# Down products of two feed-forward layers by Strassen's seven block products

## Chip, cores and metric

One core of a Trainium2 chip runs the whole program. The metric is device time in microseconds. All arithmetic that matters here is on 32-bit data; each exact product is made of three TensorE passes (high x high, low x high, high x low), where high is the rounded part of a value (type fp32r) and low what the rounding left.

## Reference

One decoder layer on 1024 prompt tokens and 64 decode tokens, D_MODEL = 1024, D_FF = 2816:

```
def _swiglu(x, w_gate, w_up, w_down):
    return (jax.nn.silu(x @ w_gate) * (x @ w_up)) @ w_down
...
    x = _layer_norm(DN_ALPHA * x + 0.5 * _swiglu(x, f1g, f1u, f1d), ln_g[0], ln_b[0])
    m, s_new, new_k, new_v = _mixer(x, w_in, w_out, gn_w, sinks, ret_state, k_buf, v_buf)
    x = _layer_norm(DN_ALPHA * x + m, ln_g[1], ln_b[1])
    x = _layer_norm(DN_ALPHA * x + 0.5 * _swiglu(x, f2g, f2u, f2d), ln_g[2], ln_b[2])
```

`_mixer` (retention and window attention between two projections) lies between the layers that are changed.

## The kernel before

`ffn_stage` is one feed-forward layer, called twice. It goes over FT = 22 feature tiles of 128. For each tile f, TensorE makes the gate and then the up product of three token chunks (362, 364 and 362 tokens; 8 k-tiles x 3 passes = 24 matmuls each, so 48 per chunk), in two pairs of PSUM banks. ScalarE takes the silu of gate, VectorE multiplies it with up (`h_full`, L539), ScalarE rounds that (L308) and VectorE makes the low part (L547, and L549 for the decode rows). `down(f)` then multiplies the hidden tile with the down weights: for 8 token tiles and two halves of 512 columns 3 matmuls of 512 columns (L459 to L461), for the decode rows 2 x 2 (L456, L457), 52 in all, through four PSUM banks. VectorE adds each of the 18 results into `acc` in SBUF (L561). In the loop, a step is gate and up of tile f, then `down(f - 1)`. The last two tiles, A and B, are interleaved by hand: their down products go together in PSUM (`last_down`, L483 to L487), tile by tile, with the layer norm's steps behind each tile (`norm_tile`: sums, ScalarE `deviation`, GpSimd `gain` (L714), VectorE `shift` (L739), TensorE `turn` (L751), ScalarE `high`, VectorE `low` (L769)).

Weights come by the one DMA queue of SyncE: gate, up and down tile of 512 KB each, requested when the down products of an earlier tile are done. ScalarE rounds each tile (`round_part`, L293), GpSimd subtracts to get its low part in place (`split`, L375, 1024 columns). During the first layer's start SyncE also loads the first two weight tiles (Q, K) of the retention projection and the norm's rows (`between_loads`); ScalarE and GpSimd round and split them there (`RetentionPrefetch`, L838 and L843). After the layer, `retention_projection_stage` loads, rounds (L900) and splits (L955) the other two, V and GATE. Every engine runs its own list in order; the list orders are those of the functions `sync`, `scalar`, `gpsimd`, `tensor`, `vector`.

Of the kernel before, what the change touches and what calls it, by code (L numbers as in the profile page):

```python
# [22 lines left out]
F32 = mybir.dt.float32  # L23
# [5 lines left out]
P = 128  # L29
# [4 lines left out]
SEQ = 1024  # L34
# [152 lines left out]
class FfnBuffers:  # L187


    def __init__(self, tag, even, odd, work):  # L190

        self.hi, self.raw, self.low = [], [], []
        for s, place in enumerate((even, odd)):
            self.hi.append([place.put(f"{tag}w_hi{s}{j}", [P, KT, P], F32R) for j in range(3)])
            pairs = [place.put_raw_and_low(f"{tag}w{s}{j}", [P, KT, P]) for j in range(3)]
            self.raw.append([raw for raw, _ in pairs])
            self.low.append([low for _, low in pairs])
        self.h_hi = [work.put(f"{tag}h_hi{s}", [P, TOK + 2 * DEC], F32R) for s in range(2)]
        self.h_lo = [work.put(f"{tag}h_lo{s}", [P, SEQ], F32R) for s in range(2)]
        self.silu = work.put(tag + "silu", [P, 3, CW])  # L200
        self.h_full = work.put(tag + "h_full", [P, 3, CW])


def ffn_stage(core, tag, buffers, w_in, fold, acc, xh, xl, wait_x, acc_ready, norm, room=None, banks_free=None,
              first_norm=None, load=None, between_loads=lambda sp: None, prefetch=None):

    w_hi, w_raw, w_lo = buffers.hi, buffers.raw, buffers.low
    h_hi, h_lo, silu, h_full = buffers.h_hi, buffers.h_lo, buffers.silu, buffers.h_full
    GATE, UP, DOWN = range(3)
    NC_ = len(CHUNKS)  # L210
    DOWNS = 2 * TOKEN_TILES
    sem = lambda n: core.semaphore(tag + n)
    gate_ps, up_ps, down_ps = core.banks[0:4:2], core.banks[1:4:2], core.banks[4:8]
    staged = [sem(f"staged{j}") for j in range(3)]
    gu_hi, down_hi = sem("gu_hi"), sem("down_hi")
    gu_split, down_split = sem("gu_split"), sem("down_split")
    gate_done, up_done = sem("gate_done"), sem("up_done")
    silu_done = sem("silu_done")
    pair_free = sem("pair_free")
    h_hi_done, h_lo_done = sem("h_hi_done"), sem("h_lo_done")  # L220
    down_done, down_free = sem("down_done"), sem("down_free")

    A, B = FT - 2, FT - 1

    LAST = [(A, 0), (A, 1), (B, 0), (B, 1), (A, 2), (B, 2)]

# [27 lines left out]

    def load_part(sp, f, s, j):
        src = w_in[f, :, j, :] if isinstance(f, int) else w_in[bass.ds(f, 1), :, j, :].rearrange("a p n -> (a p) n")
        sp.dma_start(flat(w_raw[s][j]), src).then_inc(staged[j], 16)

    def sync_early(sp, j):
        load_part(sp, 0, 0, j)  # L260

    def sync(sp):
        if room:
            sp.wait_ge(*room)
            load_part(sp, 0, 0, DOWN)
# [28 lines left out]

    def scalar_early(act, j):
        round_part(act, 0, 0, j)

    def scalar(act):
        def silu_chunk(f, s, c):
            a, b = CHUNKS[c]  # L300
            act.wait_ge(gate_done, number(f, c) + 1)
            act.activation(silu[:, buffer_of(f, s, c), 0:b - a], gate_ps[pair_of(f, s, c)][:, 0:b - a],  # L302
                           ACT.Silu).then_inc(silu_done, 1)

        def round_h(f, s, c):
            a, b = CHUNKS[c]
            act.wait_ge(pair_free, 2 + number(f, c) + 1)
            act.activation(h_hi[s][:, a:b], h_full[:, buffer_of(f, s, c), 0:b - a],  # L308
                           ACT.Copy).then_inc(h_hi_done, 1)

        def silu_and_round(f, s, c):
            silu_chunk(f, s, c)
            round_h(f, s, c)

        def step(f, s):
            silu_and_round(f, s, 0)
            round_part(act, f + 1, 1 - s, GATE)
# [5 lines left out]
        def first_step():
            silu_and_round(0, 0, 0)
            round_part(act, 1, 1, GATE)
            round_part(act, 1, 1, UP)
            silu_and_round(0, 0, 1)
            round_part(act, 0, 0, DOWN)
            silu_and_round(0, 0, 2)

        def first_step_with_norm():
            silu_chunk(0, 0, 0)
            first_norm.high(act, TOKEN_TILES - 3)
            round_h(0, 0, 0)
            first_norm.high(act, TOKEN_TILES - 2)
            round_part(act, 1, 1, GATE)
            silu_chunk(0, 0, 1)
            first_norm.high(act, TOKEN_TILES - 1)
            round_h(0, 0, 1)
            round_part(act, 1, 1, UP)  # L340
            round_part(act, 0, 0, DOWN)
            silu_and_round(0, 0, 2)

        if first_norm:
            first_step_with_norm()
        else:
            first_step()
        if prefetch:
            prefetch.scalar_early(act)
        tiles(act, step)  # L350
        round_part(act, B, 1, GATE)
        round_part(act, B, 1, UP)
        silu_and_round(A, 0, 0)
        round_part(act, A, 0, DOWN)
        silu_and_round(A, 0, 1)
        silu_and_round(B, 1, 0)
        round_part(act, B, 1, DOWN)
        silu_and_round(B, 1, 1)
        norm.deviation(act, 0)
        norm.deviation(act, 1)  # L360
        silu_and_round(A, 0, 2)
# [4 lines left out]
        silu_and_round(B, 1, 2)  # L366
# [5 lines left out]
    def split(pool, f, s, j):  # L372
        done, rounded, n = (down_split, down_hi, f + 1) if j == DOWN else (gu_split, gu_hi, 2 * f + j + 1)
        pool.wait_ge(rounded, n)
        pool.tensor_tensor(flat(w_lo[s][j]), flat(w_raw[s][j]), flat(w_hi[s][j]).bitcast(F32),  # L375
                           ALU.subtract).then_inc(done, 1)
# [5 lines left out]
    def gpsimd(pool):  # L382
        def step(f, s):
            split(pool, f + 1, 1 - s, GATE)
            split(pool, f + 1, 1 - s, UP)
            split(pool, f, s, DOWN)

        step(0, 0)
        if prefetch:
            prefetch.gpsimd_early(pool)  # L390
        tiles(pool, step)
        split(pool, B, 1, GATE)
        split(pool, B, 1, UP)
        split(pool, A, 0, DOWN)
        split(pool, B, 1, DOWN)
# [3 lines left out]
    def tensor(pe):  # L399
        def gate_or_up(f, s, c, j):  # L400
            a, b = CHUNKS[c]
            ps, done = ((gate_ps, gate_done), (up_ps, up_done))[j]
# [7 lines left out]
            mm.then_inc(done, 1)  # L410

        def first_gate():
# [14 lines left out]
            mm.then_inc(gate_done, 1)  # L427
# [7 lines left out]
        def high_and_low(s):  # L435

            return h_hi[s][:, SEQ:SEQ + P], h_hi[s][:, TOK:TOK + P]

        def down(f, s):
            pe.wait_ge(down_split, f + 1)  # L440
            for t in range(TOKEN_TILES):
                if t in (0, 2, 5):
                    pe.wait_ge(h_lo_done, number(f, chunk_of_tile(t)) + 1)
                if t == BLOCKS - 1:
                    pe.wait_ge(gu_split, min(2 * f + 6, 2 * FT) if isinstance(f, int) else 2 * f + 6)
                if t == BLOCKS:
                    pe.wait_ge(down_split, f + 2)
                u = slice(P * t, P * t + P)
                for half in range(2):
                    n, d = 2 * t + half, slice(512 * half, 512 * half + 512)  # L450
                    pe.wait_ge(down_free, DOWNS * f + n + 1 + DOWNS - 4)
                    out = down_ps[(n + 2 * s) % 4]
                    hi, lo = flat(w_hi[s][DOWN])[:, d], flat(w_lo[s][DOWN])[:, d]
                    if t == BLOCKS:
                        both = h_hi[s][:, SEQ:SEQ + P]
                        pe.matmul(out, both, hi, start=True, stop=False)  # L456
                        pe.matmul(out, both, lo, start=False, stop=True).then_inc(down_done, 1)  # L457
                    else:
                        pe.matmul(out, h_hi[s][:, u], hi, start=True, stop=False)  # L459
                        pe.matmul(out, h_lo[s][:, u], hi, start=False, stop=False)  # L460
# [1993 lines left out]
```

## Time and profile before

| | before |
|---|---|
| runs (3) | 2143.75 us median, 2142.12 to 2144.74 |
| profiled execution | 2143.15 us, its span 2141.3 us |
| TensorE busy | 2096.4 us, 98% of the span |
| VectorE, ScalarE, GpSimd busy | 910.3, 505.7 and 520.6 us |
| granted TensorE clock, mean | 0.994 of full speed |

The profile is one execution. Matmul ends in it are modelled, so the cost of a matmul is best read as the distance between the starts of two neighbours. In the rows, PE is TensorE, DVE VectorE, ACT ScalarE, POOL GpSimd, SPq the DMA queue of SyncE.

### The profile page before, as it was taken

The page shows a single profiled execution, that of the slowest core. Times are in us where ns is not written, and L with a number is a line of the kernel's source. Part 1 is how long each engine was busy: PE and PEld are TensorE (multiplying, and loading weights), DVE is VectorE, ACT ScalarE, POOL GpSimd, SP SyncE. Part 2 cuts the span into 40 slices and gives each one's busy share as a digit, 9 for nine tenths or more (in the row PEclk, how much of TensorE's full clock was granted, in tenths as well). Part 3 has the DMA queues.
Part 4 walks back from the last instruction along what each step waited for, and adds up shares of the span by engine and source line. Part 5 has one row for each costly group of instructions (what it writes and reads, how often), then busy time and mean ns, then how long its engine had stood idle before and what let it go on. Part 6 is the DMA issues. An engine that isn't in the chain of part 4 may idle for free.

```text
span 2141.3 us, 31092 instructions
## 1 busy us (share of the span) xinstructions
PE 2096.4 (98%) x11989; PEld 1927.4 (90%) x11989; DVE 910.3 (43%) x1686; ACT 505.7 (24%) x887; POOL 520.6 (24%) x261
## 2 busy tenths in 40 slices
PE   8999999999999999999998999999999999999997
PEld 8999999999999989999796667999999999999996
DVE  5534353535353552101656536444444443434346
ACT  4111111111112153111136344211111111111115
POOL 3221212121212132221454223212121212121213
PEclk9999999999999999999999999999999999999999
DMA  7010101010101112111123011110101010101012
GB/s 287 30 59 29 59 29 59 29 59 31 57 33 56 40 50 74 50 39 34 62 86 141 1 50 60 34 60 29 59 29 59 29 59 29 59 29 59 30 59 84
DMA packets 38074, 118.40 MB, mean 55 GB/s; under 512 B 6271, under 2 KB 10879, under 8 KB 37759
## 3 DMA queue, kind: packets, MB, share of 16 engines
q1 hardware_dynamic: 38015, 117.58, 15.3%
q8 instruction: 41, 0.67, 0.1%
q14 instruction: 18, 0.15, 0.0%
HBM read 106.29 MB, written 11.27 MB: 55 GB/s over the span
## 4 chain that ended last, share of the span: by engine, by line
PE 95%; DVE 2%; issue 1%; DMA 1%; ACT 1%; POOL 0%; SPq 0%; DVEq 0%; ACTq 0%
PE bank L119 20%; PE bank L121 20%; PE bank L120 20%; PE bank L461 7%; PE bank L460 7%; PE bank L459 7%; PE bank L1863 2%; PE bank L1865 2%; PE bank L1864 2%; PE bank L1833 1%; PE bank L457 1%; PE bank L456 1%; PE bank L751 1%; PE bank L486 1%; PE bank L1185 1%
## 5 line engine op out<-in xcount | busy, mean ns | idle before, releaser
L119 PE MATMUL bank<-x_hi,f_w_hi 128*128 128x362 f32 (+1 forms) x2104 | 689.2, 328 | 1.8 <-DVE x_low L162 1.8
L121 PE MATMUL bank<-x_hi,f_w_low 128*128 128x362 f32 (+1 forms) x2104 | 689.1, 328 | 0.0
L375 POOL TENSOR_TENSOR f_w_low<-f_w_raw,f_w_hi 128x1024 fp32r<-128x1024 f32 x132 | 316.6, 2415 | 1182.5 <-ACT f_w_hi L293 1182.5
L561 DVE TENSOR_TENSOR acc<-bank,acc 128x512 f32<-128x512 f32 x720 | 467.8, 686 | 6.7 <-PE bank L461 4.4
L539 DVE TENSOR_TENSOR f_h_full<-bank,f_silu 128x362 f32<-128x362 f32 (+1 forms) x132 | 70.6, 535 | 815.3 <-PE bank L121 813.0
L119 PEld LDWEIGHTS bank<-x_hi,f_w_hi 128*128 128x128 f32 x2104 | 395.9, 188 | 3.9 <-issue 2.0
L121 PEld LDWEIGHTS bank<-x_hi,f_w_low 128*128 128x128 f32 x2104 | 396.2, 188 | 0.0
L120 PE MATMUL bank<-x_lo,f_w_hi 128*128 128x362 f32 (+1 forms) x1056 | 345.5, 327 | 0.0
L120 PE MATMUL bank<-x_low,f_w_hi 128*128 128x362 f32 (+1 forms) x1048 | 343.0, 327 | 0.0
L461 PE MATMUL bank<-f_w_low,f_h_hi 128*128 128x512 f32 x640 | 250.4, 391 | 0.0
L459 PE MATMUL bank<-f_w_hi,f_h_hi 128*128 128x512 f32 x640 | 250.0, 391 | 0.3 <-DVE acc L561 0.3
L460 PE MATMUL bank<-f_w_hi,f_h_lo 128*128 128x512 f32 x640 | 250.3, 391 | 0.0
L302 ACT ACTIVATE f_silu<-bank 128x362 f32<-128x362 f32 (+1 forms) x132 | 62.5, 474 | 678.3 <-PE bank L121 678.2
L120 PEld LDWEIGHTS bank<-x_lo,f_w_hi 128*128 128x128 f32 x1056 | 198.7, 188 | 1.0
L120 PEld LDWEIGHTS bank<-x_low,f_w_hi 128*128 128x128 f32 x1048 | 197.2, 188 | 0.8
L308 ACT ACTIVATE f_h_hi<-f_h_full 128x362 fp32r<-128x362 f32 (+1 forms) x132 | 67.0, 508 | 528.6 <-DVE f_h_full L539 528.6
L461 PEld LDWEIGHTS bank<-f_w_low,f_h_hi 128*128 128x128 f32 x640 | 120.2, 188 | 25.9
L459 PEld LDWEIGHTS bank<-f_w_hi,f_h_hi 128*128 128x128 f32 x640 | 120.3, 188 | 25.3 <-DVE f_h_lo L547 0.7
L460 PEld LDWEIGHTS bank<-f_w_hi,f_h_lo 128*128 128x128 f32 x640 | 120.2, 188 | 24.5
L293 ACT ACTIVATE f_w_hi<-f_w_raw 128x1024 fp32r<-128x1024 f32 x132 | 133.9, 1044 | 33.7 <-DMA f_w_raw<-ffn_in 33.7
L119 PE MATMUL bank<-x_hi,rp_w_hi 128*128 128x362 f32 (+1 forms) x384 | 126.9, 331 | 0.0
L120 PE MATMUL bank<-x_low,rp_w_hi 128*128 128x362 f32 (+1 forms) x384 | 126.1, 328 | 0.0
(207 smaller groups left out, 2215.7 us busy)
## 6 DMA issues: line engine op xcount, KB each, us to landing
f_w_raw<-ffn_in SPq DMA_DIRECT2D x132, 512.0 KB, 4.4
rp_w_raw<-w_ret_in SPq DMA_DIRECT2D x16, 512.0 KB, 3.5
acc<-x_rows_in SPq DMA_DIRECT2D x2, 2048.0 KB, 11.1
kept_rows<-acc SPq DMA_DIRECT2D x8, 512.0 KB, 2.9
ow_raw<-w_out_in SPq DMA_DIRECT2D x8, 512.0 KB, 6.6
y_out<-acc SPq DMA_DIRECT2D x8, 512.0 KB, 2.7
n_rows<-ln_rows_in SPq DMA_DIRECT2D x6, 512.0 KB, 5.1
gp_stage<-w_att_in SPq DMA_DIRECT2D x4, 512.0 KB, 3.5
```

The source lines that it names most:

```text
L119: pe.matmul(out, wh, xh, start=first, stop=False)
L120: pe.matmul(out, wh, xl, start=False, stop=False)
L121: return pe.matmul(out, wl, xh, start=False, stop=last)
L293: act.activation(flat(w_hi[s][j]), flat(w_raw[s][j]), ACT.Copy).then_inc(down_hi if j == DOWN else gu_hi, 1)
L302: act.activation(silu[:, buffer_of(f, s, c), 0:b - a], gate_ps[pair_of(f, s, c)][:, 0:b - a], ACT.Silu).then_inc(silu_done, 1)
L308: act.activation(h_hi[s][:, a:b], h_full[:, buffer_of(f, s, c), 0:b - a], ACT.Copy).then_inc(h_hi_done, 1)
L375: pool.tensor_tensor(flat(w_lo[s][j]), flat(w_raw[s][j]), flat(w_hi[s][j]).bitcast(F32), ALU.subtract).then_inc(done, 1)
L459: pe.matmul(out, h_hi[s][:, u], hi, start=True, stop=False)
L460: pe.matmul(out, h_lo[s][:, u], hi, start=False, stop=False)
L461: pe.matmul(out, h_hi[s][:, u], lo, start=False, stop=True).then_inc(down_done, 1)
L539: dve.tensor_tensor(h_full[:, at, 0:b - a], up_ps[pair_of(f, s, c)][:, 0:b - a], silu[:, at, 0:b - a], ALU.mult).then_inc(pair_free, 1)
L561: dve.tensor_tensor(acc[:, t, d], down_ps[(n + 2 * s) % 4][:, :], acc[:, t, d], ALU.add).then_inc(down_free, 1)
```

## The change

The 22 feature tiles are worked in 11 pairs. For ten of them the 2 x 2 block product (two halves of 512 tokens by two feature tiles, times two feature tiles by two halves of 512 output columns) is made by Strassen's seven block products. Each product is a *group* of four token tiles x 3 matmuls of 512 columns; the decode rows get 8 matmuls. The five sums of hidden blocks are made by VectorE, the five sums of down weights by GpSimd; sums and blocks are rounded by ScalarE, and their low parts are subtracted by VectorE (hidden) and GpSimd (weights). VectorE adds or subtracts a product from PSUM into one or two places of `acc`. The groups of the pair before lie between half chunks (24 matmuls of gate or of up) of the current pair. The last pair (A, B) keeps `last_down`, in another order with its last chunks. Gate and up tiles are requested when the tile that held their buffer is done, down tiles two at a time when the pair's last group is done. Down tiles of the first pair are no longer loaded ahead. The prefetch of the retention weights and the norm's rows are loaded at the end of layer 1, and only Q is rounded and split there; K waits for the end of the products, and its split stands ahead of `norm.gain(7)`. Silu is written into `h_full` in place. Buffers are laid out anew. The core of the diff; first the seven products, each with its hidden block, its weight block, the parts it waits for, and its targets (rows, columns, sign):

```
+SEVEN = [
+    (H1, D1, 1, 1, [(0, 0, ADD), (1, 1, ADD)]),
+    (H2, D2, 1, 2, [(1, 0, ADD), (1, 1, SUB)]),
+    (H3, D3, 2, 3, [(0, 1, ADD), (1, 1, ADD)]),
+    (H4, D4, 3, 3, [(0, 0, ADD), (1, 0, ADD)]),
+    (H5, D5, 4, 4, [(0, 1, ADD), (0, 0, SUB)]),
+    (H6, D6, 4, 5, [(1, 1, ADD)]),
+    (H7, D7, 4, 5, [(0, 0, ADD)]),
+]
```

SyncE, for each pair q with f = 2q:

```
+            sp.wait_ge(gu_done, 12 * q)
+            load_part(sp, f + 1, 1, GATE)
+            load_part(sp, f + 1, 1, UP)
+            sp.wait_ge(gu_done, 12 * q + 6)
+            load_part(sp, f + 2, 0, GATE)
+            load_part(sp, f + 2, 0, UP)
+            sp.wait_ge(down_done, SEVENS * q)
+            load_down(sp, f, 0)
+            load_down(sp, f + 1, 1)
```

ScalarE, `round_pair`:

```
+            act.wait_ge(h_ready, (SUMS + LOWS) * q + 2)
+            high(cut(buffers.h_hi, 2, 4), cut(buffers.h_raw, 2, 4))
+            act.wait_ge(pair_free, 2 + number(f, 2) + 1)
+            high(cut(buffers.h_hi, 0, 1), h_full[:, 0, 0:HALF])
+            high(cut(buffers.h_hi, 1, 2), h_full[:, 1, HALF:SEQ])
+            act.wait_ge(down_split, (DOWN_SUMS + DOWN_LOWS) * q + DOWN_SUMS)
+            weights(cut(buffers.ds_hi, 0, 1), cut(buffers.ds_raw, 0, 1))
+            weights(cut(buffers.d_hi, 0, 1), cut(buffers.d_raw, 0, 1))
+            weights(cut(buffers.ds_hi, 1, 3), cut(buffers.ds_raw, 1, 3))
+            act.wait_ge(h_ready, (SUMS + LOWS) * q + SUMS)
+            high(buffers.hs_hi[:, :], buffers.hs_raw[:, :])
+            weights(cut(buffers.d_hi, 3, 4), cut(buffers.d_raw, 3, 4))
+            weights(cut(buffers.d_hi, 1, 3), cut(buffers.d_raw, 1, 3))
+            high(packs[:, 0:6 * DEC].rearrange("p (s n) -> p s n", s=2)[:, :, 0:DEC], h_full[:, :, SEQ:TOK])
+            high(pack(2, 0, DEC), dec_sum[:, :])
```

GpSimd, for each pair (`sums`: five of 512 columns; `split_down`: 512, 512, 1024, 512 and 1024 columns):

```
+            split(pool, f + 1, 1, GATE)
+            split(pool, f + 1, 1, UP)
+            split(pool, f + 2, 0, GATE)
+            split(pool, f + 2, 0, UP)
+            sums(q)
+            split_down(q)
```

TensorE, for each pair, with p = q - 1:

```
+            gate_up(f, 0, 0)
+            gate_up(f, 0, 1, between=lambda: group(p, 0))
+            group(p, 1)
+            gate_up(f, 0, 2, between=lambda: group(p, 2))
+            group(p, 3)
+            gate_up(f + 1, 1, 0, between=lambda: group(p, 4))
+            decode(p)
+            gate_up(f + 1, 1, 1, between=lambda: group(p, 5))
+            group(p, 6)
+            gate_up(f + 1, 1, 2)
```

VectorE, `sums_and_lows`:

```
+            dve.wait_ge(pair_free, 2 + number(f, 2) + 1)
+            combine(raw(H1), a11, a22, ADD)
+            combine(raw(H2), a21, a22, ADD)
+            combine(raw(H5), a11, a12, ADD)
+            combine(raw(H6), a21, a11, SUB)
+            combine(raw(H7), a12, a22, SUB)
+            combine(dec_sum[:, :], h_full[:, 0, SEQ:TOK], h_full[:, 1, SEQ:TOK], ADD)
+            low(1, cut(buffers.h_lo, 2, 4), cut(buffers.h_raw, 2, 4), cut(buffers.h_hi, 2, 4))
+            low(2, cut(buffers.h_lo, 0, 1), a11, cut(buffers.h_hi, 0, 1))
+            low(3, cut(buffers.h_lo, 1, 2), a22, cut(buffers.h_hi, 1, 2))
+            low(4, buffers.hs_lo[:, :], buffers.hs_raw[:, :], buffers.hs_hi[:, :])
+            low(6, two[:, :, DEC:2 * DEC], h_full[:, :, SEQ:TOK], two[:, :, 0:DEC])
+            low(6, pack(2, DEC, 2 * DEC), dec_sum[:, :], pack(2, 0, DEC))
```

VectorE, for each pair:

```
+            h_chunk(f, 0, 0)
+            add_group(p, 0)
+            h_chunk(f, 0, 1)
+            add_group(p, 1)
+            add_group(p, 2)
+            h_chunk(f, 0, 2)
+            add_group(p, 3)
+            add_group(p, 4)
+            h_chunk(f + 1, 1, 0)
+            add_decode(p)
+            add_group(p, 5)
+            h_chunk(f + 1, 1, 1)
+            add_group(p, 6)
+            h_chunk(f + 1, 1, 2)
+            sums_and_lows(q, f + 1)
```

TensorE, the last phase, from tile A on:

```
+        gate_up(A, 0, 0)
+        gate_up(A, 0, 1, between=lambda: group(p, 0))
+        two_groups(1)
+        gate_up(B, 1, 0, between=lambda: group(p, 3))
+        group(p, 4)
+        decode(p)
+        gate_up(B, 1, 1, between=lambda: two_groups(5))
+        gate_up(A, 0, 2)
         last_down(0)
         last_down(1)
```

## Rows read from the trace of the kernel before

**Rows 1.** The page: span, busy times, chain by engine, granted clock.
```profile
span 2141.3 us, 31092 instructions
PE 2096.4 (98%) x11989; PEld 1927.4 (90%) x11989; DVE 910.3 (43%) x1686; ACT 505.7 (24%) x887; POOL 520.6 (24%) x261
PEclk9999999999999999999999999999999999999999
PE 95%; DVE 2%; issue 1%; DMA 1%; ACT 1%; POOL 0%; SPq 0%; DVEq 0%; ACTq 0%
```
**Rows 2.** Waits from 100 to 740 us (us in total, times, longest).
```profile
DVE f_h_full L539 <- PE bank L121: 344.0, 53, 7.0
...
PEld bank L459 <- issue: 0.2, 1, 0.2
```
**Rows 3.** Windows on TensorE: stretch, us, busy (matmuls recorded), clock, DMA share, GB/s.
```profile
407.47:415.15 7.68, 7.68 (x49) 1.00 0.00 0
415.15:426.98 11.83, 11.83 (x55) 1.00 0.00 0
426.98:434.98 8.00, 8.00 (x50) 1.00 0.55 197
...
1527.91:1540.00 12.09, 12.09 (x54) 1.00 0.00 0
```
**Rows 4.** Instruction groups by shape: busy us, mean ns; idle before.
```profile
L561 DVE TENSOR_TENSOR acc<-bank,acc 128x512 f32<-128x512 f32 x720 | 467.8, 686 | 6.7 <-PE bank L461 4.4 <-DVE acc L561 0.2
...
L547 DVE TENSOR_TENSOR f_h_lo<-f_h_full,f_h_hi 128x362 fp32r<-128x362 f32 x44 | 24.2, 550 | 25.3 <-ACT f_h_hi L308 25.3
...
L1139 POOL TENSOR_TENSOR rt_q_dec<-ret_q,rt_q_decay 128x512 f32<-128x512 f32 x8 | 10.2, 1270 | 35.9 <-DVE ret_v_tok L1046 23.3 <-PE bank L1185 11.9 <-DMA rt_own<-own_in 0.8
```
**Rows 5.** Timeline of VectorE and GpSimd, 36 to 60 us: start, us, instruction.
```profile
38.78 2.29 DVE L167 TENSOR_SCALAR acc<-acc 128x4096 f32<-128x4096 f32 x1 [0.59 <-DMA acc<-x_rows_in]
40.99 4.52 DVE L168 TENSOR_SCALAR acc<-acc 128x4096 f32<-128x4096 f32 x1
45.44 2.89 DVE L169 TENSOR_SCALAR acc<-acc 64x1024 f32<-64x1024 f32 x1
...
54.51 2.79 DVE L547 TENSOR_TENSOR f_h_lo<-f_h_full,f_h_hi 128x364 fp32r<-128x364 f32 x1 [0.58 <-ACT f_h_hi L308]
...
40.96 6.82 POOL L843 TENSOR_TENSOR rp_w_low<-rp_w_raw,rp_w_hi 128x1024 fp32r<-128x1024 f32 x2 [7.22 <-ACT rp_w_hi L838]
52.14 7.41 POOL L375 TENSOR_TENSOR f_w_low<-f_w_raw,f_w_hi 128x1024 fp32r<-128x1024 f32 x3 [4.36 <-ACT f_w_hi L293]
```
**Rows 6.** Timeline, GpSimd and VectorE at 807 to 811 us.
```profile
807.56 2.52 POOL L714 TENSOR_TENSOR acc<-acc,n_rows 128x1024 f32<-128x1024 f32 x1 [2.33 <-ACT acc L698]
807.74 0.68 DVE L578 SCALAR_TENSOR_TENSOR acc<-bank,acc 128x512 f32<-128x512 f32 x1
...
810.20 1.28 DVE L739 SCALAR_TENSOR_TENSOR acc<-acc,n_stats,n_rows 128x1024 f32<-128x1024 f32 x1 [0.85 <-POOL acc L714]
```
**Rows 7.** DMA issues after a tile: the queue's timeline, and us to landing.
```profile
427.32 1.38 SPq L257 DMA_DIRECT2D f_w_raw<-ffn_in  x3
...
f_w_raw<-ffn_in SPq DMA_DIRECT2D x3, 512.0 KB, 4.3
```
**Rows 8.** Timeline at the end of layer 1: last weight split, table load.
```profile
749.36 2.40 POOL L375 TENSOR_TENSOR f_w_low<-f_w_raw,f_w_hi 128x1024 fp32r<-128x1024 f32 x1 [25.51 <-ACT f_w_hi L293]
...
765.46 1.28 ACT L302 ACT_TABLE_LOAD   x1
```
**Rows 9.** Timeline at the start of the retention projection.
```profile
810.79 1.04 ACT L900 ACTIVATE rp_w_hi<-rp_w_raw 128x1024 fp32r<-128x1024 f32 x1
...
812.78 3.23 DVE L739 SCALAR_TENSOR_TENSOR acc<-acc,n_stats,n_rows 128x1024 f32<-128x1024 f32 x1
816.92 0.69 DVE L769 TENSOR_TENSOR x_low<-bank,x_hi 128x512 fp32r<-128x512 f32 x1 [0.90 <-ACT x_hi L762]
...
817.76 1.60 PE L751 MATMUL bank<-small,acc 128*128 128x128 f32 x8 [2.15 <-DVE x_low L769]
```

More of the change, by code:

```diff
@@ L196, in __init__ @@
             self.raw.append([raw for raw, _ in pairs])
             self.low.append([low for _, low in pairs])
[L198 to L201, printed above, removed]
+        self.packs = pack.put(tag + "h_packs", [P, 2 * 3 * DEC + 2 * DEC], F32R)
+        self.h_full = main.put(tag + "h_full", [P, 2, TOK])
@@ L323, in first_step @@
[L323 to L332, printed above, removed]
+            if c == 0:
+                act.wait_ge(down_done, DONE - SEVENS + 16)
+            rows = min(b, SEQ)
+            x = act.activation(h_row(buffers.h_hi, s, a, rows), h_full[:, s, a:rows], ACT.Copy)
@@ L348, in scalar @@
+        round_last_down(A, 0)
+        round_last_down(B, 1)
+        round_last(B, 1, 1)
+        round_last(A, 0, 2)
         if prefetch:
             prefetch.scalar_early(act)
[L350 to L358, printed above, removed]
         norm.deviation(act, 0)
@@ L433, in gate_up @@
             gate_or_up(f, s, c, UP)
[L435 to L460, printed above, removed]
-                        pe.matmul(out, h_hi[s][:, u], lo, start=False, stop=True).then_inc(down_done, 1)
@@ new lines, in decode @@
+        def decode(q):
+            pe.wait_ge(h_ready, (SUMS + LOWS) * q + SUMS + LOWS)
+            for half, parts in enumerate((((2, D2), (1, D4)), ((2, D5), (0, D3)))):
+                n = 4 * FIFTH + half
+                pe.wait_ge(down_free, SEVENS * q + SEVENS + n - 3)
+                out = down_ps[n % 4]
+                for i, (s, which) in enumerate(parts):
+                    both = pack(s, 0, 2 * DEC)
+                    pe.matmul(out, both, slot(buffers.d_hi, buffers.ds_hi, which), start=i == 0, stop=False)
+                    mm = pe.matmul(out, both, slot(buffers.d_lo, buffers.ds_lo, which), start=False, stop=i == 1)
+                mm.then_inc(down_done, 1)
@@ L563, in add_down, with add @@
-        def add_down(f, s, ns=range(DOWNS)):
-            for n in ns:
-                add_part(f, s, n)
+                x = dve.tensor_tensor(pack(s, DEC, 2 * DEC), h_full[:, s, SEQ:TOK], pack(s, 0, DEC).bitcast(F32),
+                                      ALU.subtract)
+            x.then_inc(h_ready, 1)
+        def add(q, n, t, half, op, last):
+            d = slice(HALF * half, HALF * half + HALF)
+            x = dve.tensor_tensor(acc[:, t, d], acc[:, t, d], down_ps[n % 4][:, :], op)
+            if last:
+                x.then_inc(down_free, 1)
```

515 lines of the change are left out of this document (320 added, 195 removed).

## Prediction

> **What bounds the kernel now.** I read the page first: TensorE is busy 98% of the span at full granted clock, VectorE 43%, ScalarE and GpSimd 24% each, and the chain that ended last is TensorE for 95% [rows 1]. Then the waits of a long stretch of the first feed-forward layer: TensorE's own waits add up to 0.2 us in 640, and what the other engines wait for is mostly TensorE's results [rows 2]. So time falls where TensorE issues less, and rises where a new wait makes TensorE stop. Then come the windows, which give the cost of a matmul as the distance between starts: the 52 products of one down tile take 11.83 us, 0.2275 each; a 48-matmul chunk takes 7.68 us (0.160 each) or 8.00 (0.1667) [rows 3]. In the second layer 52 products took 12.09 us in one tile [rows 3].
>
> **What is removed.** Two feature tiles now cost 52 x 2 = 104 down matmuls. Seven block products of 4 token tiles x 3 passes are 84, and the decode rows 2 x 4 = 8: 92. That is 12 fewer for each of 10 pairs in each of 2 layers, 240 in all, at 0.2275 us: **-54.6 us**. The last pair of a layer stays as it is. Without stalls a pair would take 96 x (0.160 + 0.1667 + 0.160) + 92 x 0.2275 = 46.7 + 20.9 = 67.7 us, against two times 35.5 now (11.83 + 7.68 + 8.00 + 8.00). DMA bytes are the same. The buffers lie elsewhere, and the rate of one shape differs by 2 to 4% between places in rows 3 without my knowing why: plus or minus 10 us, taken at 0.
>
> **What is added.** Per pair, VectorE adds 48 + 2 products into `acc` instead of 36: 14 more at 0.686 us [rows 4], 9.6 us on an engine that idles over half the time. A product with two targets takes VectorE about 0.64 + 0.61 = 1.25 us and TensorE 3 x 0.2275 = 0.68; a group (2.7) with the half chunk behind it (3.8) leaves 6.5 us for 5.0 of adds, so inside a pair the adds are covered once they have begun in time. What must be in time is the block at the end of a pair, `sums_and_lows`: twelve VectorE instructions that read two SBUF tensors, and beside it five sums and five splits of down weights on GpSimd, 9 x 512 columns or 1024. Durations: 362 columns took VectorE 0.550 us, 512 took 0.686 [rows 4], 1024 took 1.28 [rows 6]; in a row of them each occupies VectorE about 0.08 less than it takes, so I count 0.61 for 512, 1.14 for 1024, 1.68 for 1536 and 0.15 for 64 or 128. The five sums of 512, the small sum, the lows of 1024, 512, 512, 1536 and the packed rows occupy VectorE 7.3 us in all. GpSimd takes 1.27 us for 512 columns [rows 4], 2.40 for 1024 [rows 8].
>
> **The two engines exclude each other there.** VectorE's 4096-column scaling took 2.29 us alone and 4.52 behind a GpSimd split that began 0.03 us before; the 1024-column one behind it took 2.89, because the second GpSimd split, waiting since, went first; the two splits took 6.82 instead of 2 x 2.40. A 364-column `h_lo` subtraction took 2.79 us instead of 0.55 under three GpSimd splits, which together took 7.41 [rows 5]. An addition from PSUM at 807.74 took its usual 0.68 under a running GpSimd instruction [rows 6]. I read this as: an instruction with two SBUF inputs waits for the end of the other engine's one, and the two then alternate. The Trainium skill, "SBUF — State Buffer", section "SBUF: two separate sides", says the same, that the pair of ports is locked for a whole instruction and the loser fully blocks; by that rule too this change is dearer than its busy times, and the trace agrees with the 2.79 and 4.52 us above; without the rule the sum would be rival 2's. In the kernel before, the meetings are rare, since splits run where VectorE adds from PSUM or idles.
>
> **The schedule of a pair, from rows.** Zero is the start of the next pair's first gate chunk. The last group ends at -7.7 (one chunk of 0.160 x 48). The DMA queue starts its issues 0.34 us after the tile's end, the second 0.47 later, and one of 512 KB landed 4.3 us after issue as the median of three [rows 7]; both down loads are there at -7.7 + 5.1 = -2.6. GpSimd's sums run from then, three of them done at +1.1. VectorE's last `h_full` ends at 0.8. From here the two alternate: sum 1 1.1 to 1.7, GpSimd's fourth to 2.8, sum 2 to 3.3, its fifth to 4.4, sums 3 to 5 to 6.1. ScalarE has rounded the first weight block at 5.9, so GpSimd takes 6.0 to 7.2; small sum to 7.3; split 2 to 8.4; the first low (1024) 8.4 to 9.5; split 3 (1024) to 11.7; low 2 to 12.2; split 4 to 13.3; low 3 to 13.8; split 5 (1024) to 16.1; low 4 (1536) to 17.6. By now ScalarE has also rounded the next gate and up tiles (0.95 each from 12.8), so GpSimd goes on with two splits of 2.3 us, and VectorE's two packed-row instructions wait for one each: it is free at **22.3**. In that order VectorE waited some 14 us for 7.3 of work. It then does `h_full` of chunk 0, which is queued behind, and only at 22.8 the first add, although TensorE gave group 0 from 11.7 to 14.4. The up half chunk covers until 18.4. Group 1 needs the banks of group 0: its products can start at 24.1, 25.4, 26.6, 27.9 and the last ends at 28.6 instead of 21.1. **Stall 7.4 us per pair.** After it the adds are in time again. The stall recurs as long as both engines have work, for pairs 2 to 10, that is 9 times in a layer; the first pair's down weights are early and it costs 0.8.
> Sum: 18 x 7.4 + 2 x 0.8 = **+134.8 us**. Bounds: if VectorE wins the fewest turns (the overlap of start-up, about 0.1 us each, taken as none) 9.5 us a pair; if the loads land 0.3 us sooner, GpSimd's fifth sum ends before sum 3 wants, the first low is done at 7.3, and one GpSimd instruction fewer stands ahead of low 4: VectorE is free at 17.8, stall 2.9. If there is no exclusion at all it is free at about 11 and the stall is 0.
>
> **The ends of the layers.** (a) In the last phase groups 1 and 2 stand back to back, paced by 1.25 us a product: 2.7 us more each layer (1.4 without exclusion). (b) The last down weights are loaded after group 6, but ScalarE rounds them behind the silu of the chunk before `last_down(0)`: gate end +3.84, silu +0.7, two roundings, two splits of 2.41, about 10.5 us after the start of a chunk that lasts 7.7: 2.8 us each layer. Before, this split ran from 749.36 to 751.8, ahead of its use at 755 [rows 8]. (c) The last silu now waits behind `deviation(3)` and a table load of 1.28 us [rows 8] while its up half is shorter: 1.9 us in the first layer, 1.3 in the second. (d) At the change to the retention projection the second weight tile (K) is rounded and split only after the last product, and its split stands ahead of `norm.gain(7)` on GpSimd. Now: gain(7) 807.56 to 810.1, then shift(7) 810.20, ending with the last shift at 816.0 and x_low at 816.92 [rows 6, 9]. After: rounding of K ends where V's ended, 811.85; its split to 814.4; gain(7) to 816.8; the splits of V and GATE, long rounded, follow it and take turns with the last three VectorE instructions of 1.28: shift(7) after V's at 819.1 to 820.2, the next after GATE's at 822.5 to 823.6, the last shift to 824.9, x_low of tile 6 to 825.7. TensorE's turn of tile 7, now at 817.76, would start at about 826.4: +8.7 us. Norm rows, prefetch and `kept_rows` stay covered; they are loads of 512 KB that have over 10 us. Sum: 5.4 + 5.6 + 3.2 + 8.7 = **+22.9**.
> At the starts nothing: down weights no longer come early and the GpSimd splits of the prefetch, under which the scaling ran slow, are gone; what TensorE waits for there is x, whose loads stand ahead as before.
>
> **Sum.** -54.6 + 134.8 + 22.9 = +103.1 us on the profiled execution's own 2143.15 us (its span is 2141.3; the median of the runs is 2143.75): **2246 us**.
>
> **Rivals.** (1) *The stall stays small*: the same alternation in its better order, 2.9 us a pair: -54.6 + 53.8 + 22.9 = +22.1, 2165 us. For it: the two orders are parted by some 0.3 us in the landing. Against: 5.1 us is the measured landing. 23%. (2) *Covered*: the sums and splits do not collide (or VectorE keeps its turn), it is free by 18.4, when group 1 needs the first bank, and the stall is 0: -54.6 + 2.8 + 5.6 + 3.2 + 8.7 = -34.3, **2109 us**, faster. It decides when VectorE leaves the block within 17 us of zero: then the count of matmuls rules. For it: VectorE has only 42 us of work in 68 (50 adds at 0.64, six `h_full` at 0.5, the block's 7.3). Against: rows 5. 22%. (3) *Between the two*, 1 to 2 us a pair, 2115 to 2150 us: 8%. (4) *VectorE becomes late through the whole pair* (9.5 us a pair, or adds of over 0.75): 2260 to 2285: 5%.
>
> **Chances and range.** The forecast 42%, its own range 2215 to 2260. Slower by over 0.2% (about 4.3 us, what this measurement can tell from none): 42 + 20 + 5 = 67%; within 0.2%: 5%; faster 28% (all of rival 2, most of 3). The range from 2105 to 2260 takes in the forecast, rivals 1 and 3 and the upper part of 2.
>
> **What the new profile would show.** Group matmuls 240 fewer at 0.227 us; VectorE additions at about 0.69; `hs` and `h` sums and lows with means far over 0.69 (waits inside); a gap on TensorE ahead of group 1, about 7 us, "idle, released by VectorE acc", once in each pair, with the period near 75 us; one gap of about 3 us ahead of the first `last_down`. I am wrong if the sums on VectorE have their bare durations, if the period is near 68, or if the gap sits at another group (then the adds, not the exclusion, are the bound).

## The result, and the profile after

The changed kernel takes 2267.87 us (median of 4 runs, 2260.48 to 2269.38) against 2144.24 us for the one before (4 runs, 2142.12 to 2146.21): a ratio of 1.057, 95% interval 1.0545 to 1.0595. It is slower, as forecast, but by 124 us instead of 103, and 8 us above the top of my range. The profiled execution is the fastest of the four, 2260.48 us.

The page of the changed kernel, beside [rows 1]: span, busy times, granted clock and the chain by engine.

```profile
span 2258.7 us, 31130 instructions
PE 2101.8 (93%) x11749; PEld 1914.3 (85%) x11749; DVE 1416.2 (63%) x2046; ACT 549.5 (24%) x947; POOL 800.9 (35%) x421
PEclk9999999999999999999999999999999999999999
PE 75%; DVE 17%; issue 6%; ACT 1%; DMA 1%; POOL 1%; DVEq 0%; SPq 0%; ACTq 0%
```

TensorE has its 240 matmuls less (11989 to 11749), yet its busy time grew by 5 us, and its share of the chain fell from 95% to 75%, with VectorE now at 17%. Over the whole run the mean granted clock is 0.965, against 0.994 before. The waits from 120 to 750 us (TensorE's own were 0.2 us in the 640 us of [rows 2]):

```profile
DVE f_h_full L689 <- PE bank L121: 113.4, 34, 7.1
...
DVE acc L736 <- PE bank L580: 57.0, 37, 4.0
...
PE bank L578 <- DVE acc L736: 41.2, 9, 6.0
```

The groups by shape, beside [rows 4]:

```profile
L736 DVE TENSOR_TENSOR acc<-acc,bank 128x512 f32<-128x512 f32 x1000 | 623.3, 680 | 149.6 <-PE bank L580 135.2 <-PE bank L592 11.5 <-DVE acc L736 0.4
...
L704 DVE TENSOR_TENSOR f_h_low<-f_h_full,f_h_hi 128x512 fp32r<-128x512 f32 x40 | 82.1, 2091 | 0.0
...
L704 DVE TENSOR_TENSOR f_hs_low<-f_hs_raw,f_hs_hi 128x1536 fp32r<-128x1536 f32 x20 | 75.7, 3785 | 3.8 <-ACT f_hs_hi L369 3.8
...
L704 DVE TENSOR_TENSOR f_h_packs<-f_h_full,f_h_packs 128x128 fp32r<-128x128 f32 x20 | 49.0, 2449 | 0.0
L578 PE MATMUL bank<-f_d_hi,f_h_hi 128*128 128x512 f32 x80 | 48.8, 611 | 99.1 <-DVE acc L736 99.0
```

The thousand additions from PSUM kept their price, 680 ns against 686 before. The instructions with two SBUF inputs did not: 2.09 us for 512 columns, 2.45 us for 128. They are long themselves and do not stand behind missing inputs: VectorE's idle time ahead of these three groups is 3.8 us in the whole run. The last line holds the stall: the products that read `d_hi` and `h_hi` are those of group 1 (4 in each of 20 pairs), and they stood 99 us behind VectorE's additions.

One pair in the timeline of VectorE and GpSimd (`f_h_packs` holds the decode rows). Its zero, the first matmul of the next pair's first gate chunk, is 433.27:

```profile
434.04 2.79 DVE L700 TENSOR_TENSOR f_h_raw<-f_h_full 128x512 f32<-128x512 f32 x2
436.75 2.98 DVE L700 TENSOR_TENSOR f_hs_raw<-f_h_full 128x512 f32<-128x512 f32 x3
439.66 1.32 DVE L700 TENSOR_TENSOR f_dec_sum<-f_h_full 128x64 f32<-128x64 f32 x1
440.91 2.33 DVE L704 TENSOR_TENSOR f_h_low<-f_h_raw,f_h_hi 128x1024 fp32r<-128x1024 f32 x1
443.16 4.58 DVE L704 TENSOR_TENSOR f_h_low<-f_h_full,f_h_hi 128x512 fp32r<-128x512 f32 x2
447.67 3.97 DVE L704 TENSOR_TENSOR f_hs_low<-f_hs_raw,f_hs_hi 128x1536 fp32r<-128x1536 f32 x1
451.56 2.44 DVE L704 TENSOR_TENSOR f_h_packs<-f_h_full,f_h_packs 128x128 fp32r<-128x128 f32 x1
453.92 2.35 DVE L704 TENSOR_TENSOR f_h_packs<-f_dec_sum,f_h_packs 128x64 fp32r<-128x64 f32 x1
456.20 0.52 DVE L689 TENSOR_TENSOR f_h_full<-bank,f_h_full 128x362 f32<-128x362 f32 x1
...
430.75 3.83 POOL L485 TENSOR_TENSOR f_ds_raw<-f_d_raw 128x512 f32<-128x512 f32 x3 [21.06 <-DMA f_d_raw<-ffn_in]
...
449.98 6.21 POOL L471 TENSOR_TENSOR f_w_low<-f_w_raw,f_w_hi 128x1024 fp32r<-128x1024 f32 x2
```

GpSimd's sums begin at -2.5 (forecast -2.6), VectorE's block starts at 0.8 (0.8) and lets `h_full` through at 22.9 (22.3). A packed row of 64 columns takes 2.35 us there, about the length of one GpSimd split of 1024 columns (2.40 in [rows 8]). TensorE in the same pair, as windows (stretch, length, busy of PE, PEld, DVE, ACT, POOL, clock, DMA share, GB/s):

```profile
451.90:457.97 6.07, 0.32 (x3) 0.02 (x2) 6.07 (x6) 0.47 (x1) 4.30 (x2) 0.95 0.00 0
457.97:460.60 2.63, 2.63 (x6) 1.98 (x7) 2.63 (x5) 0.00 (x0) 0.00 (x0) 0.50 0.00 0
460.60:466.00 5.40, 5.40 (x30) 4.78 (x30) 5.40 (x10) 0.00 (x0) 0.00 (x0) 0.98 0.00 0
```

TensorE stands still until group 1 at 457.97, 24.7 after zero (24.1). Then the granted clock is 0.50, its lower level of 1.2 GHz, after 5.8 us in which TensorE had waited. This was not in my prediction. Here it lasts 2.6 us and group 1 takes 4.39 us; in other pairs the wait is as long, the clock is at 0.50 through all of group 1, and group 1 takes 5.3 us. The interval between two blocks is 68.98 us for the first in layer 1 and 69.03 in layer 2, 70.46 once, and 76.5 to 77.9 in the other 15; behind the last block of each layer there is no next one to measure to, and group 1 waited there too.

### The profile page after: what moved, and what is told of

It is laid out like the page before. It is cut to its first block, busy times and chain, and to the rows that moved or that the text cites. A ratio compares the mean times of both kernels' runs of the same rounds, so it can differ in the third digit from the quotient of the medians.

```text
span 2258.7 us, 31130 instructions
## 1 busy us (share of the span) xinstructions
PE 2101.8 (93%) x11749; PEld 1914.3 (85%) x11749; DVE 1416.2 (63%) x2046; ACT 549.5 (24%) x947; POOL 800.9 (35%) x421
## 4 chain that ended last, share of the span: by engine, by line
PE 75%; DVE 17%; issue 6%; ACT 1%; DMA 1%; POOL 1%; DVEq 0%; SPq 0%; ACTq 0%
PE bank L119 15%; PE bank L121 15%; PE bank L120 15%; PE bank L578 6%; PE bank L579 5%; PE bank L580 5%; DVE f_h_packs L704 4%; DVE f_hs_low L704 3%; DVE f_h_low L704 2%; DVE acc L736 2%; PE bank L2076 2%; PE bank L2078 1%; PE bank L2077 1%; DVE f_hs_raw L700 1%; DVE f_h_raw L700 1%
## 5 line engine op out<-in xcount | busy, mean ns | idle before, releaser
L736 DVE TENSOR_TENSOR acc<-acc,bank 128x512 f32<-128x512 f32 x1000 | 623.3, 680 | 149.6 <-PE bank L580 135.2
L471 POOL TENSOR_TENSOR f_w_low<-f_w_raw,f_w_hi 128x1024 fp32r<-128x1024 f32 x88 | 236.4, 2705 | 514.6 <-ACT f_w_hi L354 504.7
L364 ACT ACTIVATE f_h_full<-bank 128x362 f32<-128x362 f32 (+1 forms) x132 | 62.5, 474 | 1137.4 <-PE bank L121 964.5
L689 DVE TENSOR_TENSOR f_h_full<-bank,f_h_full 128x362 f32<-128x362 f32 (+1 forms) x132 | 70.2, 532 | 314.7 <-PE bank L121 311.4
L485 POOL TENSOR_TENSOR f_ds_raw<-f_d_raw 128x512 f32<-128x512 f32 x60 | 76.1, 1297 | 380.3 <-DMA f_d_raw<-ffn_in 380.3
L578 PE MATMUL bank<-f_d_hi,f_h_hi 128*128 128x512 f32 x80 | 48.8, 611 | 99.1 <-DVE acc L736 99.0
L121 PE MATMUL bank<-x_hi,rp_w_low 128*128 128x362 f32 (+1 forms) x384 | 127.2, 331 | 0.0
L503 POOL TENSOR_TENSOR f_ds_low<-f_ds_raw,f_ds_hi 128x512 fp32r<-128x512 f32 (+1 forms) x40 | 100.2, 2505 | 52.7 <-ACT f_ds_hi L372 52.7
L503 POOL TENSOR_TENSOR f_d_low<-f_d_raw,f_d_hi 128x512 fp32r<-128x512 f32 (+1 forms) x60 | 114.7, 1925 | 0.0
L578 PE MATMUL bank<-f_ds_hi,f_h_hi 128*128 128x512 f32 x240 | 94.9, 396 | 1.9 <-DVE acc L736 1.9
```

Source lines behind the costliest of these rows:

```text
L121: return pe.matmul(out, wl, xh, start=False, stop=last)
L485: pool.tensor_tensor(out, x, y, op).then_inc(down_split, 1)
L503: pool.tensor_tensor(lo[:, u], raw[:, u], hi[:, u].bitcast(F32), SUB).then_inc(down_split, 1)
L578: pe.matmul(out, high, w_h, start=True, stop=False)
L689: dve.tensor_tensor(h_full[:, s, a:b], up_ps[pair_of(f, s, c)][:, 0:b - a], h_full[:, s, a:b], ALU.mult).then_inc(pair_free, 1)
L736: x = dve.tensor_tensor(acc[:, t, d], acc[:, t, d], down_ps[n % 4][:, :], op)
```

## The experiments

Line numbers of the variants can lie a few higher than those above. Each ratio is to the kernel before on the same chip.

### 1. GpSimd's share taken away

```
-                pool.tensor_tensor(out, x, y, op).then_inc(down_split, 1)
+                pool.tensor_tensor(out[:, 0:n], x[:, 0:n], y[:, 0:n], op).then_inc(down_split, 1)
...
-                u = slice(HALF * a, HALF * b)
+                u = slice(HALF * a, HALF * a + few if few else HALF * b)
...
-            w_h, w_l = slot(buffers.d_hi, buffers.ds_hi, d), slot(buffers.d_lo, buffers.ds_lo, d)
+            w_h, w_l = slot(buffers.d_hi, buffers.ds_hi, d), slot(buffers.d_hi, buffers.ds_hi, d)
```

`n` and `few` are 8, but for the first pair of a layer, which keeps its full widths. TensorE reads the rounded weights in place of their low parts, so this kernel leaves work out of GpSimd's share and none out of VectorE's or TensorE's.

> Work is left out: in the pairs of the loop GpSimd's five sums and five splits of down weights work on 8 columns instead of 512 or 1024, and TensorE reads the rounded weights where it read their low parts; counts of instructions and waits stay. My theory (the two engines exclude each other on instructions with two SBUF inputs) expects VectorE's block of sums and lows at 8 to 9 us instead of 22.2, no wait of TensorE ahead of group 1, the granted clock at 1.00 through the pairs, and a period of 69.0 us as in the first pair instead of 76.5 to 77.9: 18 x about 8 less, 2120 to 2130 us. The rival, that the 50 additions from PSUM are too many for VectorE, expects the wait to stay, above 2250 us. A third reading, that ScalarE's roundings set the block, expects the block above 12 us and a time between.

Measured: 2117.83 us, ratio 0.9878 (0.9861 to 0.9894) to the kernel before, 2 us below the range of my theory. Groups by shape, and one whole pair as a window:

```profile
L700 DVE TENSOR_TENSOR f_hs_raw<-f_h_full 128x512 f32<-128x512 f32 x60 | 37.8, 686 | 0.0
L704 DVE TENSOR_TENSOR f_hs_low<-f_hs_raw,f_hs_hi 128x1536 fp32r<-128x1536 f32 x20 | 37.2, 1860 | 25.1 <-ACT f_hs_hi L369 25.1
...
L704 DVE TENSOR_TENSOR f_h_low<-f_h_full,f_h_hi 128x512 fp32r<-128x512 f32 x40 | 25.8, 686 | 0.0
```

```profile
406.20:475.25 69.05, 69.05 (x382) 65.04 (x381) 42.24 (x69) 13.81 (x21) 13.75 (x14) 1.00 0.14 46
```

VectorE's instructions are untouched and have their bare durations again: 686 ns where 2091 stood, the block 9.2 us instead of 22.2, the period 69.05, the clock 1.00. With all 1000 additions in place there is no stall, so their number is not the bound. Nor are ScalarE's roundings, with which the block would have stayed above 12 us. ScalarE's `hs_hi` holds VectorE up by 1.25 us a pair (25.1 in 20), which costs TensorE nothing. The Trainium skill, "SBUF — State Buffer", section "SBUF: two separate sides", has the pair of ports locked for a whole instruction, the loser fully blocked; the trace of the changed kernel agrees with 2.35 us for 64 columns beside a 1024-column split.

### 2. Part of the block moved behind group 0's additions

```
             h_chunk(f, 0, 0)
             add_group(p, 0)
+            last_lows(p)        # low(4, ...), low(6, ...), low(6, ...) out of sums_and_lows
             h_chunk(f, 0, 1)
```

ScalarE's silu of (f, 1) then waits only for low 3, that of (f, 2) for all.

> The last three subtractions of VectorE's block (low of 1536 columns, two packed rows) are issued in the next pair, after h_full of chunk 0 and the additions of group 0; nothing is left out. If the stall comes only from what stands ahead of those additions, they begin at about 14.5 + 0.5 us after zero instead of 23, group 1 finds its banks, the stall goes, the clock stays at 1.00 and the period is 69 to 70: 2120 to 2135 us. Rival: the subtractions now wait for GpSimd's gate and up splits in the middle of the additions of groups 0 and 1, and the wait only moves to group 2, with 2 to 4 us a pair: 2160 to 2200 us. If the additions themselves were the bound, nothing changes: above 2250 us.

Measured: 2148.21 us, ratio 1.0021 (1.0012 to 1.0031), 120 us less than the changed kernel. `h_full` passes 14.6 us after zero. Periods are 70.1 to 70.9 us, and the time is 13 us above the upper end of the better expectation: VectorE in the next pair shows why.

```profile
426.13 4.86 DVE L745 TENSOR_TENSOR acc<-acc,bank 128x512 f32<-128x512 f32 x8
430.91 3.47 DVE L724 TENSOR_TENSOR f_hs_low<-f_hs_raw,f_hs_hi 128x1536 fp32r<-128x1536 f32 x1
434.30 0.28 DVE L724 TENSOR_TENSOR f_h_packs<-f_h_full,f_h_packs 128x128 fp32r<-128x128 f32 x1
434.50 0.21 DVE L724 TENSOR_TENSOR f_h_packs<-f_dec_sum,f_h_packs 128x64 fp32r<-128x64 f32 x1
...
435.08 9.64 DVE L745 TENSOR_TENSOR acc<-acc,bank 128x512 f32<-128x512 f32 x16
```

The low of 1536 columns now met GpSimd's gate and up splits (3.47 us instead of 1.86), group 1's additions began at 435.1, and three products of group 2 waited 0.4 us each for a bank: the group took 4.35 us where 2.80 is its length without waits. The granted clock stayed at 1.00. The rival's mechanism was there, at 1.0 to 1.9 us a pair instead of 2 to 4.

### 3. One target for each product

```
-            targets = SEVEN[m][4]
+            targets = SEVEN[m][4][:1]
```

> Work is left out: each product is added into one target only, so that VectorE has 28 + 2 additions in a pair instead of 48 + 2. By my theory the block is untouched at 22.2 us and only the pacing of group 0's additions is halved: products of group 1 can start 0.64 apart instead of 1.25, the stall is about 5 us instead of 7.5, and with 18 pairs and the ends the time is 2205 to 2230 us. If the number of additions were the bound, the stall would go wholly: about 2125 us.

Measured: 2250.41 us in one run. Neither number was met. Against the reading that additions are the bound it is plain: 40% of them gone, and periods still of 75.6 to 77.4. But my own theory expected 2205 to 2230. The windows of the wait and of group 1:

```profile
453.60:459.10 5.50, 0.14 (x1) 0.00 (x0) 5.50 (x5) 0.47 (x1) 4.34 (x2) 0.90 0.00 0
459.12:464.40 5.28, 5.28 (x12) 4.12 (x13) 4.15 (x7) 0.00 (x0) 0.00 (x0) 0.50 0.00 0
```

I had the stall shrink because group 1's products could follow each other 0.64 us apart. They could, as far as banks go, but the clock had fallen in the wait, and twelve matmuls took 5.28 us at 0.50 instead of 2.80. In the changed kernel banks that come free 1.25 us apart and the half clock cover the same time, so removing the first brings little: the long periods are 76.5 us in the mean instead of 77.2, and what is gained is that group 1 starts some 0.6 us sooner. I had expected about 2.5 us a pair.

### 4. The order at the ends of the layers

```
         silu_chunk(B, 1, 1)
-        silu_chunk(A, 0, 2)
         round_last_down(A, 0)
         round_last_down(B, 1)
+        silu_chunk(A, 0, 2)
...
+        norm.gain(pool, 7)
         split(pool, 0, K)
-        norm.gain(pool, 7)
```

> Two changes of order at the ends of layers, nothing left out: ScalarE rounds the last down weights ahead of the silu of chunk (A, 2), and GpSimd does gain(7) ahead of the split of K. My terms (b) and (d) were 2.8 us a layer and 8.7 us once. In the trace of the changed kernel TensorE waits 2.5 and 2.3 us at the first last down product and 5.4 + 3.0 us at the turns of tiles 7 and 8 and K, against 2.2 before. So this should give back 4.8 + 5 to 8: 10 to 13 us, 2255 to 2258 us. Rival: the waits at the change to the retention projection come from the lateness of the whole norm, and only 4 to 6 us come back: 2262 to 2264 us.

Measured: 2256.01 us (ratio 1.0521, 1.0503 to 1.0538): 11.9 less than the changed kernel by the medians, as expected. TensorE's waits, 770 to 890 us:

```profile
PE bank L578 <- DVE acc L736: 6.3, 4, 5.7
PE bank L119 <- POOL rp_w_low L1167: 3.4, 1, 3.4
PE bank L968 <- DVE acc L956: 3.1, 3, 1.1
PE bank L615 <- issue: 0.7, 1, 0.7
```

The first line is group 1 of the last pair and not an end. The wait for the last down weights fell from 2.5 to 0.7 us (in layer 2 from 2.3 to nothing) and that of 5.4 us for `x_low` is gone; the one for K's low part (3.0 before, 3.4 now) remains, since ScalarE rounds K only then.

### 5. The block's tail behind group 1, with the ends mended

As in 2, but `last_lows(p)` stands behind `add_group(p, 1)`; with the edits of 4.

> The last three subtractions of VectorE's block now stand after the additions of group 1 in the next pair, and the two changes of order at the ends (rounding of the last down weights ahead of the silu of (A, 2), gain(7) ahead of K's split) are in too; nothing is left out. With them ahead of the additions of group 1 the pairs took 70.2 to 70.9 us, and TensorE waited three times 0.4 us in group 2. If those 3.9 us of subtractions are the whole rest of the stall, the period falls to 69.0, 18 x 1.4 = 25 us, and the ends give some 10: 2148 - 35 = 2113 us, 2108 to 2120. Rival: the additions of group 2, queued behind them now, come late for group 3, and the 0.4 us waits only move there: 2135 to 2142 us.

Measured: **2106.00 us** (5 runs, 2105.38 to 2107.31), ratio 0.9825 (0.9812 to 0.9839), 37 us faster than the kernel before and 2 us below the range I had given. TensorE's waits from 120 to 750 us:

```profile
PE bank L617 <- issue: 0.8, 1, 0.8
PE bank L580 <- DVE acc L745: 0.6, 3, 0.2
```

### 6. TensorE's loop elsewhere in the program

The kernel of experiment 5 with 64 fulfilled waits ahead of `pairs(pe, step)`.

> The kernel with lows after group 1 and mended ends, with 64 further waits on TensorE's queue ahead of the loop over pairs in each layer, all long fulfilled; they only move the loop's instructions in the program. It asks what makes the same matmul start every 0.160 us in one stretch and every 0.1667 in another. If the place of an instruction in the program sets it, the borders between 0.160 and 0.1667 (in layer 1 the gate half of chunk 2 is fast, the up half slow) shift or vanish, and the period of 69.0 changes by 0.3 to 1.5 us. If data, buffers or the other engines set it, pattern and period stay (69.0) and the time is within 4 us of the kernel without the waits.

Measured: 2107.83 us (ratio 0.9832, 0.9817 to 0.9847). The period stays 69.04 and 69.10, and in layer 1 the gate half of chunk 2 takes 3.84 us and its up half 4.00, as without the waits. Only the first interval of each layer is 1.0 us longer, which is the whole of the difference. The place of the loop in the program is not the cause.

### 7. One wait more for GpSimd

```
                 pool.wait_ge(down_hi, DOWN_LOWS * q + n + 1)
+                if n == 3:
+                    pool.wait_ge(h_ready, (SUMS + LOWS) * q + SUMS + LOWS)
```

> The changed kernel with one wait more and nothing left out: GpSimd does its fourth and fifth split of down weights (needed from group 4 on) only when VectorE's block of sums and lows is done, and so also its gate and up splits behind them. If the block is long because VectorE loses turns to GpSimd, five of those turns fall away behind the third split (1.2 + 2.3 + 2 x 2.3 and what stands between), VectorE is free at 14 to 17 us after zero instead of 23, the stall goes in whole or to under 1 us and the clock stays up: 2120 to 2140 us. Rival: the order of turns doesn't matter, since both engines' work is the same in sum, or TensorE then waits for the late splits at group 4: above 2200 us.

Measured: 2121.54 us, ratio 0.9900 (0.9885 to 0.9915): this line alone makes the changed kernel 146 us faster and beats the kernel before. `h_full` passes 15.6 us after zero (14 to 17). VectorE's last lows and GpSimd's fourth and fifth split:

```profile
415.28 3.49 DVE L706 TENSOR_TENSOR f_h_low<-f_h_full,f_h_hi 128x512 fp32r<-128x512 f32 x2
418.69 1.74 DVE L706 TENSOR_TENSOR f_hs_low<-f_hs_raw,f_hs_hi 128x1536 fp32r<-128x1536 f32 x1
420.36 0.28 DVE L706 TENSOR_TENSOR f_h_packs<-f_h_full,f_h_packs 128x128 fp32r<-128x128 f32 x1
420.56 0.21 DVE L706 TENSOR_TENSOR f_h_packs<-f_dec_sum,f_h_packs 128x64 fp32r<-128x64 f32 x1
```

```profile
420.85 3.67 POOL L505 TENSOR_TENSOR f_d_low<-f_d_raw,f_d_hi 128x512 fp32r<-128x512 f32 x2 [3.24 <-DVE f_h_packs L706]
```

No work went away; GpSimd gave up its turns where VectorE was in a hurry and it was not.

### 8 to 10. The buffers of layer 1 moved

```
-    weights = Layout(nc, free)
+    weights = Layout(nc, free + 64)      # and 1984, 4032
```

The kernel of experiment 5 with this edit, once for each distance.

> The kernel with lows after group 1 and mended ends; all buffers of the first layer's weights, hidden tiles and down weights ahead of the block that lies at the end of the memory stand 64 bytes further on; nothing else differs. It asks whether their place sets which matmuls start every 0.1667 and 0.2333 us instead of 0.160 and 0.2275. If it does, the pattern in layer 1 changes and its period leaves 69.04 by 0.2 to 1.5 us, while layer 2 keeps 69.10. If not, both stay.

> The same with 1984 bytes. If the place sets the rate in steps larger than 64 bytes, this one moves the period of layer 1 (69.04) by 0.2 to 1.5 us in either direction and the one with 64 bytes doesn't; if the place has no part in it, both layers keep their periods and the time is 2106 us within 3.

> The same with 4032 bytes, nearly the size of one weight tile. With the place as the cause the period of layer 1 moves by 0.2 to 1.5 us; without, 69.04 stays and the time is 2106 us within 3.

Measured, one run each: 2111.01, 2105.27 and 2104.18 us. The starts of two successive blocks, in the kernel of 5, then with 64 bytes in layer 1 and in layer 2, then with 1984 bytes:

```profile
406.02 2.79 DVE L702 TENSOR_TENSOR f_h_raw<-f_h_full 128x512 f32<-128x512 f32 x2
475.07 3.23 DVE L702 TENSOR_TENSOR f_h_raw<-f_h_full 128x512 f32<-128x512 f32 x2
```

```profile
407.75 2.68 DVE L702 TENSOR_TENSOR f_h_raw<-f_h_full 128x512 f32<-128x512 f32 x2
477.15 2.64 DVE L702 TENSOR_TENSOR f_h_raw<-f_h_full 128x512 f32<-128x512 f32 x2
...
1583.72 2.58 DVE L702 TENSOR_TENSOR f_h_raw<-f_h_full 128x512 f32<-128x512 f32 x2
1652.82 2.59 DVE L702 TENSOR_TENSOR f_h_raw<-f_h_full 128x512 f32<-128x512 f32 x2
```

```profile
404.81 2.59 DVE L702 TENSOR_TENSOR f_h_raw<-f_h_full 128x512 f32<-128x512 f32 x2
473.47 2.69 DVE L702 TENSOR_TENSOR f_h_raw<-f_h_full 128x512 f32<-128x512 f32 x2
```

The period of layer 1 is 69.05, 69.40, 68.66, and 68.66 again with 4032 bytes, and behind the first interval the same within 0.01 us in each pair of a run; layer 2, whose buffers did not move, keeps 69.10 in all four. So one run each is enough for this reading, and the place in memory changes the period, with 64 bytes as with 1984. The times alone would not have told: 2105.27 and 2104.18 us lie within the 3 us of 2106 that I had allowed for "no part".

## Why the prediction was right and where it was wrong

**The mechanism held.** Sign, engine, place and order came as forecast: the exclusion of VectorE and GpSimd, VectorE free at 22.9 (22.3), the gap ahead of group 1 once a pair, matmuls -240. Experiment 1 shows the cause by taking it away, 7 by reordering it. The evidence ahead of the result was thinner than I wrote: of the slow instructions in [rows 5] only the `h_lo` subtraction has two SBUF inputs, the scalings of `acc` have one. And the instructions of the block add up to 7.5 us by my own prices, not 7.3. *Covered* (rival 2) was wrong, and so was what it rested on, that 42 us of work in 68 leave enough slack: the share of busy time says nothing of 14 us lost at one point. *The stall stays small* (rival 1) happened in one pair of 18, that with a period of 70.46: its block took 16.0 us and the stall was 1.4 instead of 2.9. In it GpSimd did its fourth and fifth sum in a row (209.36, 2.51 us for both), its splits began 6.9 us after the start of VectorE's block instead of 5.5, and the instructions of VectorE between them had their bare durations. A sooner landing, which my text had as the cause of such an order, does not decide it: GpSimd's sums began 3.35 us ahead of VectorE's block there, and 3.07 to 3.51 us ahead in the other 17.

**The sum.** Four terms, with what they measured:

- The matmuls, -54.6: the count is right. *Placement*, "plus or minus 10 us, taken at 0": without a stall a pair takes 69.04 and 69.10 us (experiment 5). Before it was 71.0 and about 71.6, less 12 x 0.2275 gives 68.3 and 68.9, so 10 x 0.7 + 10 x 0.2 = about +9. Experiments 8 to 10 show that the place of the buffers alone can make differences of this size; that it makes these is not shown. (The 67.7 us in my text were low for another reason too: I gave two of three chunks 0.160 each where [rows 3] have one; the sum did not use it.)
- The stall, +134.8. Experiment 7 differs from the changed kernel by the stall alone: (1.057 - 0.990) x 2143 = about 144 us, or 146 by the medians. Here is the larger absolute error, +10. Of the pair looked at, I had the last product of group 1 end at 28.6; it ended at 29.1. In other pairs group 1 took up to 5.3 us instead of the 4.4 that its banks allow, and the period was 77.9 instead of 76.5. The missing step is the clock that falls during the wait: over the 17 pairs that stalled in full, group 1 took 9.4 us more than 17 x 4.39, and the half chunks behind it some 1.6 more. The waits themselves were 4 us longer in sum than forecast. Against that stands luck: the pair in the better order saved 6 us of the profiled execution. The other three runs are 7 to 9 us longer, as they would be without such a pair, but they have no trace.
- The ends, +22.9. In experiment 7 they are what is left: -21.4 + 54.6 - 9 = +24. Term by term there (the first figure of (a) and (b) is layer 1): (a) groups 1 and 2 took 8.17 and 7.92 us instead of 5.6, +2.6 and +2.3 (2.7); (b) waits of 2.5 and 2.4 us (2.8), but after that of layer 1 the clock was at 0.50 for 2.6 us and 24 matmuls took 7.08 us instead of 5.5, while after that of layer 2 it was at 1.00 and they took 5.66; (c) 0 and 0.8 (1.9 and 1.3); (d) 5.3 - 2.2 for x_low and 3.0 for K's split, 6.1 (8.7). These add up to about 18. Of the other 6 us, 3.3 are longer waits for `mix_lo` in the mixer (7.2 against 3.9 before), where the change has no part; the rest is not located. That 24 comes so near 22.9 is in part luck.
- Together +9, +10 and +1 are the 20 us by which the difference of the medians, 123.6 us, exceeds the 103.1 of the sum (the ends are a remainder, so that it closes is no proof). **The step that failed** is thus two terms mis-sized in one direction: the placement, taken at 0 and measured at +9, and the stall, priced at full clock throughout at +134.8 and measured at 144 to 146. The range failed as well: my own upper bound of 9.5 us a pair gives 2246 + 18 x 2.1 = 2284 us, but I ended the forecast's range at 2260. The number fell into the range of rival (4), whose mechanism did not happen: behind group 1 the additions were in time again.

Open: what about an address makes a matmul 6 ns longer. I did not try to separate the buffers. Also open is why one pair of 18 took the other order.

## What to carry to other kernels

Where VectorE and GpSimd both work from SBUF, count turns and not busy time: a 64-column instruction costs a whole GpSimd instruction when it queues behind one, so put what is urgent ahead of what is small, and let GpSimd wait where it has slack. One such wait was worth 146 us here, and moving three instructions behind the additions that free the banks about 150 (162 with the ends, which gave 12). When TensorE will wait some 6 us, as here, price what follows at half clock, and when two delays cover each other, removing one shows little. Last, buffers in another place moved the stall-free period by up to 0.7 us (68.66 to 69.40), a quarter of what 12 matmuls save, so measure that period before a small count is trusted.

## What the runs showed of the hardware

- The place of the operands in SBUF moves TensorE's rate at full granted clock with nothing else changed: 64 bytes +0.35 us a pair, 1984 or 4032 bytes -0.39 us, in about 380 matmuls. For one shape the spacing is 0.160 or 0.1667 us (362 columns), about 0.227 or 0.233 (512), in some stretches a mix. The place in the program changed nothing (experiment 6), and in layer 1 the pattern stayed without GpSimd's work (69.05, experiment 1). It is not a matter of the address alone: in layer 2 the 24 matmuls behind group 1 took 4.00 us without a stall and 3.92 behind one.
- With TensorE idle for 5.4 to 5.8 us the granted clock came back at 0.50, for 2.6 us in one pair of the changed kernel and for the 5.3 us of group 1 in others, as in experiment 3. Behind a wait of 2.5 us in experiment 7 it was 0.50 once, and behind one of 2.4 us 1.00. The waits of 0.4 us in experiment 2 left it at 1.00.
- VectorE's additions with one PSUM input took 679 to 686 ns in all of these kernels, GpSimd busy or not.
- Where VectorE and GpSimd both had instructions from SBUF queued, they took turns one by one in 17 of 18 pairs; in the other GpSimd had two turns in a row.
